# A two-block transformer kernel on one Trainium2 core: the first modulation's sums taken by feature tile in place of halves, with X loaded ahead of them

## What is computed

```python
sh_a, sc_a, ... = split(silu(c) @ w_ada[0] + b_ada[0], 6)        # for x
csh_a, csc_a, ... = split(silu(c_ctx) @ w_ada[0] + b_ada[0], 6)  # for ctx
hc = rmsnorm(ctx, norm_mix) * (1 + csc_a) + csh_a
hx = rmsnorm(x,   norm_mix) * (1 + sc_a)  + sh_a
u = concat(hc, hx) @ w_in          # split into qk, v, o, gates, q_a, k_a, v_a
...                                # mLSTM + window attention, out projection, conv-GLU
...                                # second block: retention + SSD layer, latent-attention layer, two SwiGLUs
return rms_norm(h_lat, final_norm_w)
```

## Time and profile before

| what | value |
|---|---|
| three runs | 1456.93 us median, 1454.11 to 1457.94 |
| the profiled execution | span 1454.6 us from its first to its last instruction; its own time is not given apart, and the span lies within the three runs, 2.3 us under their median |
| PE busy | 1403.6 us, 96% of the span |
| PE weight loads | 1172.3 us, beside the matmuls |
| DVE busy | 848.5 us, 58% |
| ACT busy | 659.0 us, 45% |
| POOL busy | 840.2 us, 58% |
| DMA | 242 MB, 166 GB/s in the mean |
| first 1/40 of the span (36 us) | PE busy 5 tenths, DMA 9 tenths, 365 GB/s |
| the other slices | PE busy 9 tenths, but the last with 8 |

### The profile page before, as it was taken

How to read it: one execution, slowest core, us unless ns; L and a number is a source line. 1 busy time by engine, 2 the same in 40 slices (tenths; PEclk the granted TensorE clock), 3 DMA queues, 4 the chain that set the end, 5 groups by cost and what they waited for, 6 DMA issues and landing times.

```text
span 1454.6 us, 21621 instructions
## 1 busy us (share of the span) xinstructions
PE 1403.6 (96%) x8272; PEld 1172.3 (81%) x8272; DVE 848.5 (58%) x1638; ACT 659.0 (45%) x1070; POOL 840.2 (58%) x672
## 2 busy tenths in 40 slices
PE   5999999999999999999999999999999999999998
PEld 2978789999988888546878888888888866888887
DVE  3798667776676689688675333321126768554522
ACT  3555665455453133684342232232226386544442
POOL 1533427998864444675444554544446530699997
PEclk9999999999999999999999999999999999999999
DMA  9748516777775652010445555533333320365664
GB/s 365 288 164 309 195 50 212 248 258 241 243 259 194 202 192 80 31 44 15 174 174 182 195 202 185 193 122 96 102 107 102 110 94 16 118 200 188 187 187 135
DMA packets 71207, 242.01 MB, mean 166 GB/s; under 512 B 7488, under 2 KB 12992, under 8 KB 70720
## 3 DMA queue, kind: packets, MB, share of 16 engines
q1 hardware_dynamic: 68688, 236.63, 48.1%
q10 hardware_dynamic: 2416, 4.00, 0.9%
HBM read 238.50 MB, written 1.05 MB: 165 GB/s over the span
## 4 chain that ended last, share of the span: by engine, by line
PE 52%; DVE 4%; ACT 1%; issue 0%; POOL 0%; DVEq 0%; ACTq 0%
PE bank L731 9%; PE bank L737 9%; PE bank L732 9%; PE bank L593 8%; PE bank L594 4%; PE bank L584 2%; PE bank L586 1%; PE bank L585 1%; PE bank L592 1%; PE cond_a L1124 1%; PE bank L1124 1%; DVE h_both L2239 1%; PE bank L1132 1%; PE cond_a L1185 1%; PE bank L1144 1%; PE cond_b L1144 1%
## 5 line engine op out<-in xcount | busy, mean ns | idle before, releaser
L2010 POOL TENSOR_TENSOR w_lo<-raw,w_hi 128x512 fp32r<-128x512 f32 (+2 forms) x610 | 776.8, 1302 | 581.1 <-ACT w_hi L1466 572.9
L1466 ACT ACTIVATE w_hi<-raw 128x1024 fp32r<-128x1024 f32 (+3 forms) x300 | 307.9, 1029 | 582.7 <-PE bank L737 375.2
L731 PE MATMUL bank<-h_both,w_hi 128*128 128x512 f32 (+1 forms) x1000 | 323.1, 340 | 1.2 <-ACT w_hi L1466 1.2
L732 PE MATMUL bank<-h_both,w_hi 128*128 128x512 f32 (+1 forms) x1000 | 322.5, 340 | 0.0
L731 PEld LDWEIGHTS bank<-h_both,w_hi 128*128 128x128 f32 x1000 | 188.3, 188 | 22.9 <-ACT w_hi L1466 1.4
L732 PEld LDWEIGHTS bank<-h_both,w_hi 128*128 128x128 f32 x1000 | 188.3, 188 | 21.3
L737 PE MATMUL bank<-h_both,w_lo 128*128 128x512 f32 (+1 forms) x1000 | 198.1, 340 | 0.0
L737 PEld LDWEIGHTS bank<-h_both,w_lo 128*128 128x128 f32 x1000 | 160.4, 188 | 21.4 <-POOL w_lo L2010 0.2
L2124 DVE CUSTOM_DVE_ANT_0 ada_junk<-ada_w,cond_a 128x1024 bf16<-128x1024 f32 x128 | 153.5, 1215 | 15.1 <-DVE work L2687 8.1
L2106 DVE TENSOR_TENSOR hidden_both<-work,hidden_both 128x256 fp32r<-128x256 f32 (+1 forms) x66 | 58.5, 886 | 135.0 <-ACT hidden_both L1547 135.0
L593 PE MATMUL bank<-h_both,w_hi 128*128 128x512 f32 x345 | 122.8, 394 | 0.0
(11 more groups left out here) (487 smaller groups left out, 2544.1 us busy)
## 6 DMA issues: line engine op xcount, KB each, us to landing
raw<-in_up SPq DMA_DIRECT2D x132, 512.0 KB, 3.6
ada_w<-in_ada SPq DMA_DIRECT2D x128, 512.0 KB, 4.5
raw<-in_down SPq DMA_DIRECT2D x48, 448.0 KB, 3.5
raw<-in_out SPq DMA_DIRECT2D x24, 512.0 KB, 3.5
raw<-in_down SPq DMA_DIRECT2D x24, 512.0 KB, 3.6
raw<-in_in SPq DMA_DIRECT2D x24, 512.0 KB, 3.5
arena<-in_ada SPq DMA_DIRECT2D x16, 512.0 KB, 11.8
raw<-in_uq SPq DMA_DIRECT2D x12, 384.0 KB, 3.1
```

Of the source, the lines that this page charges most:

```text
L731: pe.matmul(out, w_h[:, k - k0], hi[:, k, cols], start=(k == 0), stop=False)
L732: pe.matmul(out, w_h[:, k - k0], lo[:, k, cols], start=False, stop=False)
L1466: act.activation(part_slot(w_hi, f, u), raw_slot(f, u), ACT.Copy).then_inc(s["rounded"], 1)
L2010: pool.tensor_tensor(part_slot(w_lo, f, u)[:, a:b], raw_slot(f, u)[:, a:b], part_slot(w_hi, f, u)[:, a:b].bitcast(F32), ALU.subtract).then ...
```

## The change

- **Layout by feature tile.** Loads 2k and 2k+1 of `first_ada` now hold all 1024 inputs for feature tile k alone, shift and scale of its 128 features (`_tiles_of_first`). The bytes and the number of loads are the same.
- **Order of loads.** Both halves of X and the table go ahead of all `first_ada` loads; then loads 0 to 5, the two `va_gates` slots, loads 6 to 15, and the rest as before. Loads 2k and 2k+1 count on one semaphore.
- **PE.** `ada_tile(k)` (8 matmuls) and `ada_columns(k)` (2 matmuls of 2 columns against `pair_sum`, a sum of four strips of `ident`) stand eight times in place of 16 chunks and 2 column steps. Tiles 0 and 1 run ahead of the norm's sums, tile 2 behind the spread, and tile k+2 directly ahead of the projection's tile k for k = 1 to 5. The projection's 12 matmuls of a tile are split: for token tiles 0 and 1 four that need `h_hi` alone, then two with `h_lo`; then `ada_columns(k+2)`; then the same for token tiles 2 and 3.
- **ACT** does the copy of the sums (`first_rows`), which was DVE's: rows 0 and 1 between the squares and the root, row 2 ahead of the two weight roundings and of shift 0, row k+2 ahead of shift k for k = 1 to 5.
- **DVE** has `first_sums` (four small instructions that make `pair_sum` and `first_bias`) ahead of the squares' sums, and `first_modulation(k)`, two small instructions for each tile, ahead of `scaled(k)`.
- `in_halves`, `two_halves` and `sum_of_halves` are renamed, with no other edit.

```diff
-            load_first_ada(0, 3)
             sp.dma_start(X[:, :, L0:L1], dram["x"]).then_inc(s["x_in"], 16)
             sp.dma_start(X[:, :, 0:L0], dram["ctx"]).then_inc(s["x_in"], 16)
             sp.dma_start(fixed[:, :], dram["table3"]).then_inc(s["fixed_in"], 16)
-            load_first_ada(3, 8)
+            load_first_ada(0, 6)
...
-                        load_first_ada(8, 16)
+                        load_first_ada(6, 16)
...
+            def ada_tile(k):
+
+                if k >= 2:
+                    pe.wait_ge(s["ada_rows"], k - 1)
+                for half in range(2):
+                    q = 2 * k + half
+                    if half == 0 or k == KD - 1:
+                        pe.wait_ge(first_ada_in[k + (q == 2 * KD - 1)], 16 if k == KD - 1 else 32)
+                    for g in range(4):
+                        last = pe.matmul(bank[3 + k % 2][32 * g:32 * g + 32, 0:LAT], cond_t[:, 4 * half + g, :],
+                                         first_ada[:, q, g * LAT:(g + 1) * LAT], start=(half == 0), stop=(half == 1))
+                last.then_inc(s["ada_sums"], 1)
+
+            def ada_columns(k):
+
+                pe.wait_ge(s["ada_rows"], k + 1)
+                if k >= 2:
+                    pe.wait_ge(s["ada_taken"], k)
                 for j in range(2):
-                    last = pe.matmul(out[:, j], ada_rows[:, half, j * P:(j + 1) * P], picked, start=True, stop=True)
+                    last = pe.matmul(bank[6 + k % 2][:, 2 * j:2 * j + 2], ada_rows[:, k, j * P:(j + 1) * P],
+                                     pair_sum, start=True, stop=True)
                 last.then_inc(s["ada_cols"], 1)
...
+                def columns_of(k, tiles):
...
+                    gate(k, "h_round")
+                    for i in tiles:
...
+                        pe.matmul(out, h_hi[:, k, i * P:(i + 1) * P], w_h, start=(k == 0 and i % 2 == 0), stop=False)
+                        pe.matmul(out, h_hi[:, k, i * P:(i + 1) * P], w_l, start=False, stop=False)
                     gate(k)
+                    for i in tiles:
...
+                        last = pe.matmul(out, h_lo[:, k, i * P:(i + 1) * P], w_h, start=False,
+                                         stop=(k == KD - 1 and i % 2 == 1))
...
+                for k in range(KD):
+                    if 1 <= k and k + 2 < KD:
+                        ada_tile(k + 2)
+                    columns_of(k, range(TT // 2))
+                    if 1 <= k and k + 2 < KD:
+                        ada_columns(k + 2)
+                    columns_of(k, range(TT // 2, TT))
...
             pe.wait_ge(s["cond_t_ready"], 1)
-            for q in range(KD):
-                ada_chunk(q)
+            ada_tile(0)
             pe.wait_ge(s["fixed_in"], 16)
+            ada_tile(1)
             token_sums(0, TOK)
+            pe.wait_ge(s["ada_taken"], 1)
             ada_columns(0)
+            ada_columns(1)
             spread_inverse(0, TOK)
+            ada_tile(2)
+            ada_columns(2)
             first_linear(next_h())
...
+            def first_work(k):
+
+                if k == 0:
+                    first_rows(2)
+                    round_next()
+                    round_next()
+                elif k + 2 < KD and k >= 1:
+                    first_rows(k + 2)
+
             squares(0, TOK)
+            first_rows(0)
+            first_rows(1)
             rms_std(0, TOK)
-            round_next()
-            round_next()
-            shift_h(0, 0, True)
+            shift_h(0, 0, True, first_work)
...
+            def first_modulation(k):
+
+                dve.wait_ge(s["ada_cols"], k + 1)
+                dve.tensor_scalar(mod[:, 0, k, :], bank[6 + k % 2][:, 0:2], S("b_ada0")[:, k:k + 1], None, ALU.add)
+                then(dve.tensor_scalar(gain[:, 0, k, :], bank[6 + k % 2][:, 2:4], first_bias[:, k:k + 1],
+                                       S("norm_mix")[:, k:k + 1], ALU.add, ALU.mult))
+                dve.nop().then_inc(s["ada_taken"], 1)
...
                 scaled(0)
                 for k in range(1, KD):
-                    if first and k == KD // 2:
-                        lower(k - 1)
-                        first_rows(1)
-                        first_modulation(1)
+                    if first and k > 1:
+                        first_modulation(k)
                     scaled(k)
-                    if not first or k != KD // 2:
-                        lower(k - 1)
+                    lower(k - 1)
                 lower(KD - 1)
```

More of the change, by code:

```diff
@@ L314, in build @@
         c = Carve(arena, 0, limit(0))
-        first_ada, cond_t, ada_rows = c(16, 1024), c(KD, 32), c(2, LAT)
+        first_ada, cond_t, ada_rows = c(16, 1024), c(KD, 32), c(KD, LAT)
+        pair_sum, pair_tmp, first_bias = c(2), c(2), c(KD)
         c = Carve(arena, 0, limit(1))
@@ L383, in build @@
         ada_full = [sem(f"ada_full{i}") for i in range(SLOTS)]
-        first_ada_in = [sem(f"first_ada_in{i}") for i in range(16)]
+        first_ada_in = [sem(f"first_ada_in{i}") for i in range(KD + 1)]
         all_units = [(ph[n], u) for n in run for u in range(ph[n].units)]
@@ L586, in three, with two_tiles_of_first @@
                 return pe.matmul(out, w_l, x_h, start=False, stop=last)
-            def two_halves(out, w_h, w_l, x_both, first, last):
+            def two_tiles_of_first(out, w_h, w_l, x_both, first, last):
                 if last:
@@ L677, in first_linear @@
                 f = ph["va_gates"]
-                chunks = {0: (8, 9, 10, 11), 2: (12, 13, 14, 15)}
-                for k in range(KD):
-                    for q in chunks.get(k, ()):
-                        ada_chunk(q)
-                    if k == 2:
-                        ada_columns(1)
+                def columns_of(k, tiles):
                     u, n = divmod(k, KD // 2)
@@ L746, in unit @@
                         weights = w_h[:, k - k0], w_l[:, k - k0]
-                        if in_halves(name, u // parts):
-                            last = two_halves(bank_of(t), *weights, both[:, :, k, cols], k == 0, k == K - 1)
+                        if in_tiles_of_first(name, u // parts):
+                            last = two_tiles_of_first(bank_of(t), *weights, both[:, :, k, cols], k == 0, k == K - 1)
                         else:
@@ L1092, in some @@
                     for k in range(k0, k1):
-                        last = two_halves(bank_of(f.first_taken + u), w_h[:, k], w_l[:, k], h_both[:, :, k, late],
+                        last = two_tiles_of_first(bank_of(f.first_taken + u), w_h[:, k], w_l[:, k], h_both[:, :, k, late],
                                           k == 0, k == KD - 1)
@@ L1532, in round_h, with shift_h @@
                 h_count[0] += KD
-            def shift_h(n, which, both):
+            def shift_h(n, which, both, ahead=None):
                 for k in range(KD):
+                    if ahead:
+                        ahead(k)
                     act.wait_ge(s["h_work"], h_count[0] + k + 1)
@@ new lines, in first_sums @@
+            def first_sums():
+                dve.wait_ge(s["fixed_in"], 16)
+                dve.wait_ge(s["small_in"], 16)
+                dve.tensor_tensor(pair_tmp, ident[:, 0:2], ident[:, 32:34], ALU.add)
+                then(dve.tensor_tensor(pair_sum, ident[:, 64:66], ident[:, 96:98], ALU.add))
+                dve.tensor_scalar(first_bias, S("b_ada0")[:, 8:16], 1.0, None, ALU.add)
+                then(dve.tensor_tensor(pair_sum, pair_sum, pair_tmp, ALU.add))
+                dve.nop().then_inc(s["ada_taken"], 1)
@@ L2215, in norm @@
                 n = layer[0]
-                if first:
-                    first_rows(0)
-                else:
+                if not first:
                     round_third(third)
@@ L2725, in swiglu @@
                 f = ph[f"up{n}"]
-                for i in range(KF if in_halves(f.name, 0) else 0):
+                for i in range(KF if in_tiles_of_first(f.name, 0) else 0):
                     product_in(f, 2 * i)
-                    sum_of_halves(f, 2 * i, work[:, i % 3, L0:L1])
+                    sum_of_tiles_of_first(f, 2 * i, work[:, i % 3, L0:L1])
                     if i:
@@ L2736, in swiglu @@
                        .then_inc(s["hid_in"], 1)
-                for i in range(0 if in_halves(f.name, 0) else KF):
+                for i in range(0 if in_tiles_of_first(f.name, 0) else KF):
                     carried(f, 2 * i)
@@ L3054, in _ @@
             dve.wait_ge(s["x_in"], 32)
+            first_sums()
             add_squares(0, TOK)
```

67 lines of the change are left out of this document (21 added, 46 removed).

## The result

| | before | after |
|---|---|---|
| median of 4 runs | 1455.94 us | 1479.08 us |
| lowest to highest | 1454.11 to 1457.94 | 1471.65 to 1482.32 |
| span of the profiled execution | 1454.6 | 1474.9 (its time 1476.7) |
| `ka` starts | 46.74 | 66.85 |

The ratio is 1.015, interval 1.012 to 1.018. I had forecast 1467.4 with a range of 1461 to 1473, so the sign is right and the size is half of what came: +23 us by the medians, +20.3 by the spans.

What follows compares the result with a forecast made beforehand. PE, full late in the program, was taken to pay whatever its head loses: `ka` would start at 57.3, not 46.74, so 1456.9 + 10.5 = 1467.4 us, range 1461 to 1473.

Steps and rivals of the forecast that it cites:

- Landings: Loads at the head: the last still lands at about 35.4, X at about 11.1 instead of 14.96.
- The norm's chain: From X's landing over ACT, DVE and PE: root at 20.55 in place of 23.63, a gain of 3.1 us.
- Start of the projection: From PE's spread through tile 2's sums, copy, roundings, shift and `lower(0)`: projection tile 0 done at 28.4.
- The ring: Projection steps k = 1 to 5 on PE, ACT and DVE: nothing within a step overlaps, 4.97 us each; 80 in 100.
- PE behind `lower`: In each step, two matmuls 0.24, the turn to columns 0.47 and six matmuls 0.72, together 1.43 us.
- hand-overs: Between engines in each step: four of about 0.05, 0.20 us.
- a step: One projection tile to the next: sums, copy, shifts, `lower`, PE's part and hand-overs in series, 4.97 us.
- the rate of the steps: PE in the five projection steps: all taken at the fast rate, 24.85 us together.
- The tail: From the fifth step's end at 53.25 through tiles 6 and 7 to `ka` at 57.3.
- Rival 3: Behind `ka`: the head is later but the rest takes it up, price between 0 and +10; 3 in 100.
- The bounds: Low and high cases for `ka`: step 4.3, start 53, +6.2 us; step 5.4, start 60.4, +13.7 us.
- Rival 2: PE's slow rate comes back in steps and tail, 1.83 us more a step, +22 us, 1479; 6 in 100.

Runs made afterwards that it cites:

- e1: The changed kernel with two filler matmuls behind each tile's sums, where PE waits for ACT; 1471.35 us, ratio 1.0129.
- e2: The changed kernel with ACT's copy of tile k+2 behind shift k instead of ahead of it; 1463.65 us, ratio 1.0062.
- e5: The changed kernel with three first_ada loads back ahead of X, as before; 1483.45 us, ratio 1.0173.
- e12: The changed kernel with both weight roundings ahead of tile 2's copy on ACT and three filler matmuls ahead of tile 0; 1468.6 us, ratio 1.0082.
- e10: The kernel before with loads 8 to 15 in two groups of two tiles, X ahead, and three filler matmuls ahead of chunk 0; 1455.33 us, ratio 0.9989.
- e3: e2 with PE's turn of tile k+2 to columns also ahead of tile k's matmuls on `h_lo`; 1466.39 us, ratio 1.0069.
- e13: e12 with e1's two filler matmuls in each of PE's waits for ACT too; 1467.18 us, ratio 1.0074.
- e4: The kernel before with only X and the table loaded ahead of all first_ada loads; 1457.12 us, ratio 1.0009.
- e8: The kernel before with loads 8 to 15 laid out as two groups of two tiles in place of one of four; 1457.04 us, ratio 1.0001.
- e11: The kernel before with X ahead and three filler matmuls ahead of chunk 0; 1456.35 us, ratio 0.9997.

## Why the prediction was half right

**Landings: right.** X at 10.90 for 11.1, and no load is waited for behind 17 us.

**The norm's chain: right up to the root,** at 20.46 for 20.55. The path there is not the one forecast, though: the table load ended at 20.26, and the root waited 0.20 more for the norm's matmuls, 1.97 long in place of 1.10.

**Start of the projection: wrong, 28.4 for 32.27.** The step of this part that failed is "PE spreads until 22.1, sums tile 2 in 1.08". It was spread until 23.9 and tile 2's sums took 1.94. The turn to columns of tiles 0 and 1 ahead of the spread took 1.67 of that time. I took the fast rate for these since before has it from 21.91 on the earlier trace rows; the changed kernel did not have it. ACT's copy then ended at 26.26 for 23.7, and shift 0 ended at 28.4 for 26.0. PE also waited 1.51 for POOL, whose splitting waits for the roundings behind that copy, but this wait was over before `lower(0)` had ended. `lower(0)` took 1.80 beside POOL's splitting, where I had 1.3 and the earlier trace rows 1.57, and PE's eight matmuls behind it 2.00 in place of 1.05.

**The ring: right, term by term, at the fast rate.** Its terms in e1, from 43.30 to 48.15, with ACT's from the changed kernel:

| term | forecast | measured |
|---|---|---|
| sums | 1.08 | 1.07 |
| copy until the shift starts | 0.48 | 0.28 |
| two shifts | 0.91 | 0.89 |
| `lower` | 0.87 | 0.88 |
| PE behind `lower` | 1.43 | 1.57 (46.58 to 48.15) |
| hand-overs | 0.20 | 0.16, what is left of 4.85 |
| a step | 4.97 | 4.85 to 4.88 |

The copy lasts 0.38, and the shift starts 0.28 after it started; that was 0.20 less than forecast, and PE's part 0.14 more, so the sum is nearer than its terms. That ACT's order is what closes the ring is shown by e2, which changes only this order: 3.16 a step without a wait.

**What failed: the rate of the steps.** I took all five steps at the fast rate, arguing that PE is busy for over half of each and had kept the rate through waits of 0.65. The sum was therefore 24.85 for five steps; it was 30.48. From 36 to 48 us PE was busy for 9.70 of 12 us and had 0.57 of the clock, so my argument did not hold. At the slow rate a step is 7.01 (45.23 to 52.24), which is 2.24 over the last one, 4.77; I had priced 1.83. I had left out that the turn to columns slows down too (0.71 from its start to the next matmul for 0.36), and that the four matmuls on `h_hi`, slowed down, outlast `lower` (0.09). The waits did not lose the rate in every step: e5 and e12 have steps of 4.85 to 4.88 with the same waits.

**The tail: right,** 4.10 (62.75 to 66.85) for 4.1. **Nothing is given back later:** the span less `ka`'s start is 1407.9 in before and 1408.05 after. Over all 14 profiles it lies between 1404.3 (e10) and 1411.0 (e3) and does not fall with a later `ka` (1408.8 in e1, 1408.3 in e12, 1406.3 in e5). Rival 3 is out; a difference of 3 us between two single profiles behind `ka` says nothing.

So of `ka`'s 20.1 us, 9.55 were not forecast: 3.87 in the start, 5.63 in the steps and 0.05 in the tail. e13 bears the division out: it starts `ka` 10.96 earlier than after, 5.40 of it ahead of tile 3's sums and 5.56 in the four steps behind them. What part of the 5.40 is the clock's and what the roundings' place is not told apart; PE's wait there is 1.51 in after and 0.83 (for `lower(0)`) in e12.

**The bounds.** Their terms add up to a slow step of 5.29 (4.97, 0.20 for the hand-overs, 0.12 for the copy), not 5.4, and the upper end to about 59.8, not 60.4. Of the slow rate they had tile 2's sums alone, so they could not hold what came.

Rival 2 had 6 in 100 and was the case, though not as priced: I had 9.15 for the steps, 2.4 for the tail and nothing for the start, and it was 5.63, 0.05 and, with the other terms of the start, 3.87. I had made it an alternative to the forecast, with "busy for over half of each step" against it. The rows before held a warning: the half rate from 16.80 to 21.7 with waits of only 0.2 between chunks. The Trainium skill (TensorE: Matmul & The Clock Gate, Part 1) describes a PE that idles briefly between groups of matmuls as going back and forth between the two clocks. The trace of the changed kernel agrees, with sums of 1.94, 1.94, 1.94, 1.07 in a row; e1 agrees from the other side.

## What to carry to other kernels

Where two engines' ordered streams each put the next item's first stage ahead of this item's last one, the pipeline closes into a ring and a step costs the sum of its stages; add that sum up before giving each engine's busy share any weight, and try the order that finishes the item first (here 4.87 against 3.16 a step). Where an edit makes PE wait in every step, the price of the lower clock in those steps (here 2.24 for one wholly at the half rate) belongs into the forecast's own range, not into a rival of 6 in 100. And work that is cut finer has its own price on PE, which stands when the ring and the slow rate are both gone.

## What the runs showed of the hardware beside this

- **The clock's row does not show the half rate ahead of the first rise.** The granted clock reads 1.00 from 12 to 36 us in the changed kernel, where a tile's sums (8 matmuls, 16 records) take 1.94; later they take 1.07 with the same 1.00. It is so in e4 and e8 as well (1.00 with chunks of 1.08). In e2 the durations show a first rise at 26.45 and a fall at 30.4, and there the row follows: 0.74 from 28 to 32 us, 0.50 from 32 to 40. Ahead of the first rise durations tell the rate, the row doesn't.
- **The rate does not follow from the kernel alone.** e8 has before's order on PE up to 23 us, and its chunk at 22.13 takes 1.08, where before has 0.64 at 21.91. In the changed kernel PE worked from 14.03 to 25.8 with one wait over 0.5 (0.62) and stayed at 1.2 GHz, while the three matmuls without a reader (2.48 us) were followed by the fast rate in all five profiles that have them, by 16.4 to 18.2 us. The changed kernel's four runs spread over 10.7 us, and their order in time is roughly that of their mean granted clocks, from 0.991 (1471.65) to 0.984 and 0.982 (1482.32 and 1481.46). Which work earns the rate and which waits lose it stays open: with chunks of 0.64 and waits of 0.64 to 0.65 between them e10 lost it at 22.46, and e11 (18.15 to 22.0) and before (34.16 and 35.45) kept it; waits of 1.3 in the ring lost it in some steps and kept it in others.
- **Idle matmuls are no free remedy.** They took 4.9 us off `ka` and 7.7 off the median in e1, with intervals that just overlap, but in before, whose end is set by a landing, they changed nothing (e11).
